# Attention block of a decoder trunk on one NeuronCore: unscaled probabilities, weight splits in quarters, rotary angles made in the first feed-forward block, rotation moved to VectorE, output projection spread over the softmax steps

## What is computed

```python
qkv = h @ w_in + b_in
q, k = partial_rope(q, cos, sin), partial_rope(k, cos, sin)
scores = einsum('bnqhgd,bnkhd->bnhgqk', qb, kb) * (ATTN_HEAD_DIM ** -0.5)
m = maximum(max(scores, axis=-1, keepdims=True), sink)
p = exp(scores - m)
probs = p / (sum(p, axis=-1, keepdims=True) + exp(sink - m))
o = einsum('bnhgqk,bnkhd->bnqhgd', probs, vb)
return o @ w_out + b_out
```

## Time and profile before

| | |
|---|---|
| median of 3 runs | 1062.25 us (1062.09 to 1063.34) |
| profiled execution, its own time | 1062.27 us |
| its span, first to last instruction | 1060.5 us |
| PE busy | 1037.3 us, 98% of the span |
| DVE, ACT, POOL busy | 602.9, 533.6, 68.0 us |

### The profile page before, as it was taken

One profiled execution on the slowest core, in us unless ns is written; L12 is line 12 of the kernel. 1 busy time (PEld: TensorE's weight loads), 2 busy tenths in 40 slices (PEclk: granted clock), 3 DMA queues, 4 the chain that ended last, 5 costly groups with the idle time before them and its releaser, 6 DMA issues.

```text
span 1060.5 us, 14343 instructions
## 1 busy us (share of the span) xinstructions
PE 1037.3 (98%) x5304; PEld 872.5 (82%) x5304; DVE 602.9 (57%) x824; ACT 533.6 (50%) x808; POOL 68.0 (6%) x143
## 2 busy tenths in 40 slices
PE   9999999987999999999999999899999999999997
PEld 7888888864788888888888888799999988888886
DVE  5645454568655454545645554567587566455543
ACT  7444353555563443535444353477567545443532
POOL 0000000153000000000000000502202200000000
PEclk9999999999999999999999999999999999999999
DMA  9754555441156555553664555423143146555521
GB/s 326 235 195 159 213 220 179 155 155 41 55 177 217 186 164 214 215 184 112 219 199 158 208 216 184 141 91 120 41 160 114 47 159 221 195 160 211 215 87 40
DMA packets 123694, 174.67 MB, mean 165 GB/s; under 512 B 7280, under 2 KB 97664, under 8 KB 123648
## 3 DMA queue, kind: packets, MB, share of 16 engines
q1 hardware_dynamic: 120976, 171.73, 47.3%
q10 hardware_dynamic: 2672, 2.32, 0.7%
HBM read 172.98 MB, written 1.05 MB: 164 GB/s over the span
## 4 chain that ended last, share of the span: by engine, by line
PE 92%; DVE 4%; ACT 2%; POOL 1%; issue 1%; ACTq 0%; POOLq 0%; DVEq 0%
PE bank L1434 27%; PE bank L1436 27%; PE bank L1435 27%; PE bank L1738 2%; PE bank L1508 2%; PE bank L1732 2%; PE bank L1709 1%; PE bank L1465 1%; DVE prob L1217 1%; ACT w_hi L664 1%; PE bank L1648 0%; DVE w_lo L1022 0%; PE bank L1832 0%; DVE sm_max L1203 0%; DVE x_sb L1043 0%
## 5 line engine op out<-in xcount | busy, mean ns | idle before, releaser
L1022 DVE TENSOR_TENSOR w_lo<-w_raw,w_hi 128x2048 fp32r<-128x2048 f32 x159 | 362.0, 2295 | 150.5 <-ACT w_hi L664 150.5
L664 ACT ACTIVATE w_hi<-w_raw 128x2048 fp32r<-128x2048 f32 x159 | 301.5, 1918 | 114.5 <-PE bank L1436 114.0
L1434 PE MATMUL bank<-w_hi,xT_hi 128*128 128x512 f32 x784 | 310.1, 396 | 1.0 <-DVE w_lo L1149 0.7
L1436 PE MATMUL bank<-w_hi,xT_lo 128*128 128x512 f32 x784 | 305.7, 390 | 0.0
L1435 PE MATMUL bank<-w_lo,xT_hi 128*128 128x512 f32 x784 | 305.2, 389 | 0.0
L1434 PEld LDWEIGHTS bank<-w_hi,xT_hi 128*128 128x128 f32 x784 | 147.2, 188 | 32.9 <-issue 2.2
L1436 PEld LDWEIGHTS bank<-w_hi,xT_lo 128*128 128x128 f32 x784 | 147.1, 188 | 30.9
L1435 PEld LDWEIGHTS bank<-w_lo,xT_hi 128*128 128x128 f32 x784 | 147.4, 188 | 29.6 <-issue 0.2
L706 ACT ACTIVATE silu_g<-bank,rstd 128x256 f32<-128x256 f32 x88 | 37.0, 472 | 247.0 <-PE bank L1436 246.9
L1434 PE MATMUL bank<-w_hi,hT_hi 128*128 128x512 f32 x352 | 138.0, 392 | 0.0
L1436 PE MATMUL bank<-w_hi,hT_lo 128*128 128x512 f32 x352 | 137.1, 389 | 0.0
(11 more groups left out here) (287 smaller groups left out, 977.5 us busy)
## 6 DMA issues: line engine op xcount, KB each, us to landing
w_raw<-in_ffn_w_gate_up SPq DMA_DIRECT2D x170, 512.0 KB, 4.6
w_raw<-in_ffn_w_down SPq DMA_DIRECT2D x88, 512.0 KB, 4.1
w_raw<-in_gdn_w_in SPq DMA_DIRECT2D x32, 512.0 KB, 4.4
w_raw<-in_attn_w_in SPq DMA_DIRECT2D x12, 512.0 KB, 4.1
w_raw<-in_attn_w_out SPq DMA_DIRECT2D x8, 512.0 KB, 4.1
w_raw<-in_gdn_w_out SPq DMA_DIRECT2D x8, 512.0 KB, 3.9
w_raw<-in_ffn_w_gate_up SPq DMA_DIRECT2D x12, 256.0 KB, 5.6
x_sb<-in_x SPq DMA_DIRECT2D x4, 256.0 KB, 5.2
```

Source lines behind the costliest of these rows:

```text
L664: act.activation(w_hi[u0 % RING][:], w_raw[u0 % RING][:], ACT.Copy).then_inc(hi_ready, 1)
L1022: dve.tensor_tensor(w_lo[u0 % RING][:], w_raw[u0 % RING][:], w_hi[u0 % RING][:].bitcast(F32), ALU.subtract).then_inc(split_ready, 1)
L1434: pe.matmul(out_ap, a[0], b[0], start=start, stop=False, **kw)
L1436: return pe.matmul(out_ap, a[1], b[0], start=False, stop=stop, **kw)
```

## The change

- **Angles.** The positions' DMA, the angle computation on DVE and the sine on ACT move from the start of the attention into the down projection of the first FFN (after its units 0, 3 and 5). ACT loads its table for exponentials at the attention's start with one small `Exp`.
- **Rotation.** DVE rotates k and the first half of q; POOL keeps the second half of q. v is no longer padded, and only k's tiles are zeroed.
- **Unscaled probabilities.** Transposes of the probabilities wait for the exponentials themselves. PV now has the transposed probabilities as weights and v's 64 columns as moving operand, so its result has tokens as rows. DVE scales 512 columns of that by the inverse sums once in four items (`ROW_STEP`), PE transposes them (`o_transposes_att`, four transposes per group, 16 in all), and the hi and lo parts follow (`HI_STEP`, `LO_STEP`). The sink's offset and exponential and the inverse are made once per four items.
- **Splits by quarters.** Units 6 to 9 are split in four pieces of 512 columns, one per step 0 to 15.
- **Triples.** Four, not ten, of q's second half stand before the first score, twelve in steps 0 to 3. Of the output projection twelve stand in steps 11 to 18 (other banks, `ATT_ACC`), 20 behind the loop.
- **Output bias.** DVE adds it in four pieces at steps 14 to 17; before, POOL did it in two.

```diff
-A_LOADS = G_LOADS = 4
+A_LOADS, G_LOADS = 3, 4
...
-Q_BIAS_STEP, Q_STEP = 5, 7
-Q_FIRST, Q_PARTS = 10, [2, 1, 1, 1, 1]
-OUT_FIRST, OUT_PARTS = 12, [1] * 6 + [2]
+Q_BIAS_STEP, Q_STEP = 4, 7
+Q_FIRST, Q_PARTS = 4, [3, 3, 3, 3]
...
-OUT_STEP = [i + 4 for i in OUT_LAST]
+OFF_STEP = OUT_LAST
+SINK_STEP = [i + 1 for i in OUT_LAST]
+INV_STEP = [i + 2 for i in OUT_LAST]
+ROW_STEP = [i + 4 for i in OUT_LAST]
+TURN_STEP = [i + 5 for i in OUT_LAST]
+HI_STEP = [i + 6 for i in OUT_LAST]
+LO_STEP = [i + 7 for i in OUT_LAST]
+BIAS_STEP = 14
+PIECE_STEP = {6: 0, 7: 4, 8: 8, 9: 12}
+OUT_PARTS = {11: [(0, 1, 0, 0)], 12: [(0, 1, 0, 1)], 13: [(0, 1, 1, 0)], 14: [(0, 1, 1, 1)],
+             15: [(1, 1, 0, 0)], 16: [(1, 1, 0, 1)], 17: [(1, 1, 1, 0), (0, 0, 0, 0), (0, 0, 0, 1)],
+             18: [(1, 1, 1, 1), (0, 0, 1, 0), (0, 0, 1, 1)]}
...
         ACC = [(6, 7), (0, 1)]
+        ATT_ACC = [(6, 0), (7, 1)]
...
-                pool.wait_ge(k_row, t + 1)
-                after(rotate(k_pad[t][:, :, 0, 0:DH], t, HKV))
-                pool.tensor_copy(k_pad[t][:, :, 1, DH:P], k_pad[t][:, :, 0, 0:DH]).then_inc(k_rot, 1)
-                pool.wait_ge(v_row, t + 1)
-                pool.tensor_copy(v_pad[t][:, :, 1, DH:P], v_pad[t][:, :, 0, 0:DH]).then_inc(v_both, 1)
...
-            pool.wait_ge(a_loaded, 16 * A_LOADS)
-            for t in range(TT):
-                pool.wait_ge(xT_psum, 4 * E_ATT + 4)
-                pool.wait_ge(ssq_ready, TT * (E_ATT + 1))
-                pool.tensor_tensor(x_sb[:, t, :], x_sb[:, t, :], b_out[:], ALU.add).then_inc(bias_added, 1)
+                pool.wait_ge(q_biased, TT + t + 1)
+                rotate(y_sb[:, t, BANK:D].rearrange("p (h d) -> p h d", d=DH), t, BANK // DH).then_inc(q_rot, 1)
+                pool.wait_ge(q_rot, TT + t + 1)
...
+            def piece_hi_part(n, j):
+                u0 = U_ATT + n
+                act.wait_ge(raw_loaded[u0 % RING], raw_wait(u0, 0))
+                act.wait_ge(unit_done, u0 - RING + 1)
+                at = slice(j * BANK, (j + 1) * BANK)
+                act.activation(w_hi[u0 % RING][:, at], w_raw[u0 % RING][:, at], ACT.Copy).then_inc(
+                    piece_hi if j < 3 else hi_ready, 1)
...
+                    if f == 0 and d == 0:
+                        act.dma_start(pos_i[:], positions.rearrange("o (t p) -> p (o t)", p=P),
+                                      allow_slow_non_contiguous=True).then_inc(pos_loaded, 16)
+                    if f == 0 and d == 5:
+                        act.wait_ge(angle_ready, 1)
+                        act.activation(sincos[:].rearrange("p s t h r -> p (s t h r)"),
+                                       ang[:].rearrange("p s t a -> p (s t a)"), ACT.Sin).then_inc(rope_ready, 1)
...
-            act.wait_ge(angle_ready, 1)
-            act.activation(sincos[:].rearrange("p s t h r -> p (s t h r)"),
-                           ang[:].rearrange("p s t a -> p (s t a)"), ACT.Sin).then_inc(rope_ready, 1)
+            act.activation(spare[:], norm_cols[:, 0:1], ACT.Exp)
...
-            for s in range(STEPS + 1):
+            for s in range(STEPS + 3):
+                for n, (c, t) in enumerate(OUTS):
+                    if s == HI_STEP[n]:
+                        act.wait_ge(oT_psum, n + 1)
+                        act.activation(a_oT_hi[:, 4 * c:4 * c + 4, t * P:(t + 1) * P],
+                                       bank[2 * c + t][:].rearrange("p (k n) -> p k n", k=4),
+                                       ACT.Copy).then_inc(o_hi_ready, 1)
...
-                        act.activation(pr[:, h, 0:keys], bank[6 + s % 2][:, h * keys:(h + 1) * keys], ACT.Exp,
-                                       scale=DH ** -0.5, bias=sm_nmax[:, s, h:h + 1], accum_out=sm_sum[:, s, h:h + 1])
-                    act.activation(sm_sink[:, s, :], sm_off[:, s, :], ACT.Exp).then_inc(exp_done, 1)
+                        z = act.activation(pr[:, h, 0:keys], bank[6 + s % 2][:, h * keys:(h + 1) * keys], ACT.Exp,
+                                           scale=DH ** -0.5, bias=sm_nmax[:, s, h:h + 1],
+                                           accum_out=sm_sum[:, s, h:h + 1])
+                    z.then_inc(exp_done, 1)
+                for n in range(len(OUTS)):
+                    if s == SINK_STEP[n]:
+                        act.wait_ge(off_ready, n + 1)
+                        act.activation(sm_sink[:, 4 * n:4 * n + 4, :], sm_off[:, 4 * n:4 * n + 4, :],
+                                       ACT.Exp).then_inc(sink_done, 1)
...
-                if s == Q_STEP + 1:
-                    split_hi(U_ATT + 7)
-                for n, (c, t) in enumerate(OUTS):
-                    if s == OUT_STEP[n]:
-                        act.wait_ge(pv_done, OUT_PV[n])
-                        act.activation(a_oT_hi[:, 4 * c:4 * c + 4, t * P:(t + 1) * P],
-                                       bank[2 * c + t][:].rearrange("p (k n) -> p k n", k=4),
-                                       ACT.Copy).then_inc(o_hi_ready, 1)
-            for n in range(8, 10):
-                split_hi(U_ATT + n)
+                for n, first in PIECE_STEP.items():
+                    if first <= s < first + 4:
+                        piece_hi_part(n, s - first)
...
+            def piece_lo_part(n, j):
+                u0 = U_ATT + n
+                at = slice(j * BANK, (j + 1) * BANK)
+                if j < 3:
+                    dve.wait_ge(piece_hi, 3 * (n - 6) + j + 1)
+                else:
+                    dve.wait_ge(hi_ready, u0 + 1)
+                z = dve.tensor_tensor(w_lo[u0 % RING][:, at], w_raw[u0 % RING][:, at],
+                                      w_hi[u0 % RING][:, at].bitcast(F32), ALU.subtract)
+                if j == 3:
+                    z.then_inc(split_ready, 1)
...
+                    if f == 0 and d == 3:
+                        angles()
...
-            for r in range(ROT):
...
+            split_lo(U_ATT + 4)
...
+            dve.wait_ge(rope_ready, 1)
+            def rotate(v, t, heads):
+                r1, r2 = v[:, :, 0:ROT], v[:, :, ROT:2 * ROT]
+                sin, cos = sincos[:, 0, t, 0:heads, :], sincos[:, 1, t, 0:heads, :]
+                m = [r[:, 0:heads, :] for r in rot]
+                dve.tensor_tensor(m[0], r1, cos, ALU.mult)
+                dve.tensor_tensor(m[1], r2, sin, ALU.mult)
+                dve.tensor_tensor(m[2], r2, cos, ALU.mult)
+                after(dve.tensor_tensor(m[3], r1, sin, ALU.mult))
+                dve.tensor_tensor(r1, m[0], m[1], ALU.subtract)
+                return dve.tensor_tensor(r2, m[2], m[3], ALU.add)
...
-            split_lo(U_ATT + 4)
+                after(row(k_pad[t][:, :, 0, 0:DH], t, 0))
+                after(rotate(k_pad[t][:, :, 0, 0:DH], t, HKV))
+                dve.tensor_copy(k_pad[t][:, :, 1, DH:P], k_pad[t][:, :, 0, 0:DH]).then_inc(k_rot, 1)
+            for t in range(TT):
+                row(v_rows[t][:], t, HKV * DH).then_inc(v_row, 1)
...
+            for t in range(TT):
+                q_bias(0, (t,))
+                dve.wait_ge(q_biased, t + 1)
+                rotate(y_sb[:, t, 0:BANK].rearrange("p (h d) -> p h d", d=DH), t, BANK // DH).then_inc(q_rot, 1)
+                dve.wait_ge(q_rot, t + 1)
...
-                    dve.tensor_tensor(sm_off[:, s, :], sink[:, 2 * p:2 * p + 2], sm_nmax[:, s, :],
-                                      ALU.add).then_inc(max_ready, 1)
-                if 0 < s <= len(ITEMS):
-                    i = s - 1
-                    t, p = ITEMS[i]
-                    keys = (t + 1) * P
-                    dve.wait_ge(exp_done, i + 1)
-                    after(dve.tensor_tensor(sm_total[:, i, :], sm_sum[:, i, :], sm_sink[:, i, :], ALU.add))
-                    after(dve.reciprocal(sm_inv[:, i, :], sm_total[:, i, :]))
-                    for h in range(2):
-                        z = dve.tensor_scalar(prob[i % PROBS][:, h, 0:keys], prob[i % PROBS][:, h, 0:keys],
-                                              sm_inv[:, i, h:h + 1], None, ALU.mult)
-                    z.then_inc(prob_ready, 1)
-                if s == Q_BIAS_STEP:
-                    q_bias(1)
-                if s == Q_STEP + 2:
-                    split_lo(U_ATT + 7)
...
+                    four = slice(4 * n, 4 * n + 4)
+                    if s == OFF_STEP[n]:
+                        dve.wait_ge(max_ready, s + 1)
+                        dve.tensor_tensor(sm_off[:, four, :], sm_nmax[:, four, :],
+                                          sink[:, 8 * c:8 * c + 8].rearrange("p (i h) -> p i h", h=2),
+                                          ALU.add).then_inc(off_ready, 1)
+                    if s == INV_STEP[n]:
+                        dve.wait_ge(exp_done, OUT_LAST[n] + 1)
+                        dve.wait_ge(sink_done, n + 1)
+                        after(dve.tensor_tensor(sm_total[:, four, :], sm_sum[:, four, :], sm_sink[:, four, :], ALU.add))
+                        after(dve.reciprocal(sm_inv[:, four, :], sm_total[:, four, :]))
```

(87 more changed lines are left out.)

## The result

The changed kernel takes 1055.57 us (median of 4 runs, 1054.82 to 1056.67), the kernel before 1062.80 beside it (4 runs, 1062.09 to 1063.62). The ratio is 0.9936, with an interval (95%) of 0.9924 to 0.9948. The forecast was 1055.7. The profiled execution took 1054.87 us with a span of 1053.2; before, 1062.27 and 1060.5. It is one of the two fast ones of the four: those at 1056.26 and 1056.67 us ran at a mean clock of 0.997, the profiled one at 0.999.

What follows compares the result with a forecast made beforehand. PE was taken as the bound, busy 1037.3 of 1060.5 us. Terms of 73.6 plus 1.0 us gave 74.6 against 81.2, 6.6 us less, so 1062.27 became 1055.7 us; range 1052.8 to 1059.8.

Steps and rivals of the forecast that it cites:

- The walk: Step-by-step pricing of the attention in PE's instruction order, with starts from the timeline; it summed to 73.6 us.
- the stretch: Time from the end of units 0 to 3 to the next FFN's first matmul; forecast 74.6 us against 81.2.
- Start to first score: From the end of units 0 to 3 to the first score: 8.5 us, with q late on DVE.
- Steps 0 to 3: First four loop steps, scores and twelve triples: 10.8 us, no stall.
- Steps 4 to 7: Four t1 scores, three PV and transposes, 9.1 us, plus stalls of 0.8 and 1.6: 11.5 us.
- Steps 8 to 11: Four t0 scores, three PV, transposes and a triple, 7.3 us, plus stalls of 0.2: 7.5 us.
- Steps 12 to 18: Four t1 scores, six PV, transposes and eleven triples: 20.3 us, no stall over 0.1.
- Behind the loop: After the last step, 20 triples and the transposes: 15.0 us.
- Changes of kind: PE switching kinds of work, where not in the prices: 0 to 2 us more, 1.0 taken.
- the rival of short matmuls: PV at 0.72 us per fill and no cost for changes of kind: 1053.1 us; chance 0.12.
- the slower rival: Split pieces on ACT and DVE delay items PE waits for, 1.1 us per step, twelve steps: 1068.9 us; chance 0.04.
- the chain did not stay: Rival: DVE's pieces delay POOL's q rotation, step 7 waits 2 us more, another 2 us go: 1059.7 us; chance 0.14.

Runs made afterwards that it cites:

- experiment 11: Changed kernel with each product with v covering only the first 32 of a head's 64 channels: 1056.52 us, ratio 0.9938.
- Experiment 9: Kernel of experiment 2 with 16 transposes of the identity, whose result nobody reads, in the gap where the clock fell: 1057.95 us, ratio 0.9954.
- experiment 1: Changed kernel with probabilities scaled item by item on DVE again, and the sink's offset and exponential per item: 1063.29 us, ratio 1.0001.
- Experiment 12: Kernel before the change with one edit, DVE instead of POOL adding the output bias, behind the loop: 1062.77 us, ratio 1.0004.
- experiment 5: Changed kernel with the angles computed at the start of the attention again: 1062.20 us, ratio 0.9996.
- experiment 2: Changed kernel with the output bias added on POOL again, right behind its rotation of q's second half: 1059.50 us, ratio 0.9968.
- experiment 3: Changed kernel with both probabilities scaled per item on DVE and the output bias on POOL again: 1066.62 us, ratio 1.0035.
- 4: Changed kernel with units 6 to 9 split whole again instead of in quarters: 1059.63 us, ratio 0.9969.

## Why the prediction was right, and where it was not

**The sum.** The walk had 73.6 + 1.0 us for the stretch, and it is 73.95. It was made for the profiled execution, which took 1054.87 us for 1055.7; that the median of 1055.57 lies nearer is luck. By its terms, walked and measured from PE's starts:
- Start to first score: 8.5, measured 7.57. The one term that is off by more than 0.5 us. DVE's work came 0.9 to 1.1 us earlier than walked (k tiles at 216.3 and 217.9, q tiles at 222.66 and 224.5), mostly since unit 4's split began at 212.48, not at 213.2. q's first tile was ready ahead of PE, where a wait of 0.9 had been walked. The order was right: q on DVE is late, as forecast.
- Steps 0 to 3: 10.8, measured 11.0. Steps 4 to 7: 11.5, measured 11.9, with stalls of 0.72 and 1.42 where 0.8 and 1.6 were walked. Steps 8 to 11: 7.5, measured 7.7. Steps 12 to 18: 20.3, measured 20.3. Behind the loop: 15.0, measured 15.5.
- Changes of kind: 1.0 us was taken without a place for it. The steps and the part behind the loop exceed their terms by 1.3 us together, which the early start of 0.9 nearly makes up for. So the total came out better than its terms.
- The range: the terms' own bounds add up to 1053.2 to 1058.5, not to 1053.7 to 1058.3. The stated range holds both.

**The parts' prices.** Six rotation operations take 0.82 us (k) and 1.03 (q) for 0.9 and 1.1. A PV fill takes 0.84 us, inside 0.72 to 0.90; experiment 11 shows that fewer columns bring no more, and the rival of short matmuls falls. No PE wait ends with a piece, so the slower rival falls as well; at most 0.2 us of the wait of 0.72 come from one, ahead of item 5's maximum. POOL's second rotation ended at 245.06. Pieces held up three of its twelve operations by 0.3 us, so the chain did not stay. The first FFN got no gap for the angles: the attention's units 0 to 3 end at 218.43, for 218.51 before. The next FFN began at 292.38, for 293.

**What was wrong: what each part is worth.** The prediction said that no clock was won back, and for the two profiled executions that is so (1.00 in all three windows before and after). But it had no term for a clock that is lost. The changed kernel needed none, since its longest wait in the stretch, walked at 1.6 us and measured at 1.42, left the clock at 1.00; the prediction gives no reason why it should. To that extent the right total is luck. The expectations for the four dear parts were all too small: expected 2 to 3 and measured 8.2 (probabilities), 1 to 2 and 4.75 (bias), 1 to 2.5 and 4.9 (pieces), 3.5 to 4.5 and 5.9 (angles). Experiment 9 shows that the clock is the reason for 3.1 of the 4.75, and the same matmuls timed at both levels give 2.9 us for the probabilities and 2.0 for the pieces. For the angles it is nothing, though the clock fell there too; the missing term is ACT's sine and second table load ahead of unit 4's split. What then stays of experiment 1 (5.3 us) is the path of the scaling itself, 3.5 us of idle time among it, against the 3.6 that the earlier trace rows name; some 1.8 us of it I can't assign to single waits. The "slower" rival was priced without the clock too: a piece of 1.1 us in front of two waits in a row could have cost more than its own length. No run shows that case.

**No part has a value of its own.** Undone one at a time, the seven parts cost 8.2, 4.75, 4.9, 5.9, 0.7, -0.7 and 0.3 us, 24 in all, and the change brings 7.3. Three of the four dear ones lengthen a wait that exists anyway, in front of q's second half or of a PV just ahead of it, and the angles make a new one in front of k. The clock falls in or behind each of these, and in three of the four that is paid for. Experiment 12 shows the other side: done alone, the bias on DVE brings 1.3 us in the stretch and nothing in the median.

## What to carry to other kernels

Price a stall on TensorE by what it does to the clock as well: walk the longest gap of the changed kernel, and where one grows past those that the trace shows at full clock, add the work behind it at half speed, but only as far as the next wait that doesn't move: in experiment 5 such a wait swallowed all of it. Walk PE's instruction order with starts from the timeline instead of adding up idle time, and test what a part is worth both taken out and put in alone. Keep long POOL operations on two SBUF tensors away from a chain of DVE operations that read SBUF, however tiny, and read the source of such an operation's duration from its neighbour's end.

## What the runs showed of the hardware that I had not expected

- The granted clock fell from 1.00 to 0.50 (2.4 to 1.2 GHz) where PE stood still for 2.03 us (experiment 1), 3.04 (2), 2.77 (3, with 4.26 right behind it), 2.09 (4, with shorter waits around it) and 3.75 (5). In 1 and 2 it fell within the wait, in 3, 4 and 5 it fell 0.8, 1.8 and 0.6 us after PE had gone on. It stayed low for about 7 us in 1, 2 and 4, for 10 in 3 and for 3 in 5. It stayed at 1.00 after the longest gap in the stretch of the changed kernel, 1.42, and of the profiled execution before, 1.84. Sixteen idle transposes in the gap kept it at 1.00. The Trainium skill (TensorE: Matmul & The Clock Gate, Part 1: The HAM clock gate) has a throttle as the default, which activity releases; the rows at 0.50 and 1.00 agree with that.
- The same gap doesn't always have the same effect: at the start of the DeltaNet layer the clock showed 0.71 in one window of experiment 9 and stayed at 1.00 in the profiled executions of all other kernels, with the same waits of 1.9 and 1.4 us. What decides it there stays open.
- POOL's addition of two SBUF tensors held DVE operations on 2 and 8 numbers per partition for 1.79 us each (experiment 2), and none that read PSUM. Nor must a held operation read two SBUF tensors: the scaling of probabilities reads one and was held in experiment 3 (2.92 us for 0.76) and in the kernel before (4.60 for 0.62).
- Matmuls with a weight load of 128 columns each take 0.98, 1.00 and 1.06 us per eight for 32, 64 and 128 columns.
